# Expert rows of a mixture-of-experts layer: scaled and added in memory into two sums per token, in place of being stored singly and summed afterwards

## The reference, cut to what matters

```
scores = sigmoid(hf @ router_w);  e_idx = top-8 of the masked, biased scores
gate   = scores at e_idx, divided by their sum, * 2.5
yb     = (silu(xb @ w_gate[e]) * (xb @ w_up[e])) @ w_down[e]      # 128-row blocks, one expert each
routed = segment_sum(yb * row_gate, row_tok)                      # 8 rows per token
ffn    = routed + (silu(hf @ sh_gate) * (hf @ sh_up)) @ sh_down
x      = layer_norm(1.189 * x + g2 * ffn) * ln2_g + ln2_b
```

## Time and profile before

| | |
|---|---|
| three timed runs, median (lowest to highest) | 3164.0 us (3163.98 to 3166.07) |
| profiled execution: its own time | 3163.8 us |
| its span, first to last instruction | 3162.2 us |
| mean granted TensorE clock | 0.989 of full speed |
| PE busy; VectorE; ScalarE; GpSimd | 97%; 59%; 18%; 8% |
| DMA traffic | 566.57 MB, mean 179 GB/s |

### The profile page before, as it was taken

The page is one execution under the profiler, slowest core; times in us unless marked ns, Lnnn a source line. Parts: engine busy times, 40 slices in busy tenths (PEclk is TensorE's granted clock), DMA queues, the critical chain, the costliest instruction groups (busy, mean ns, idle before and its releaser), DMA issues. The chain is left out here.

```text
span 3162.2 us, 39915 instructions
## 1 busy us (share of the span) xinstructions
PE 3057.7 (97%) x12530; PEld 1759.4 (56%) x12531; DVE 1856.5 (59%) x3939; ACT 561.5 (18%) x1282; POOL 245.3 (8%) x377
## 2 busy tenths in 40 slices
PE   7999999999999899999998898999999999999998
PEld 4765667644437433333333444478844688588543
DVE  6766676666537644334333567665557755665667
ACT  1002222210002122222221225410000233200000
POOL 1000000011100122222222100000000000000000
PEclk9999999999999999999999999999999999999999
DMA  7673232378762479999997521122254334122342
GB/s 224 198 225 95 66 100 60 107 252 274 242 227 100 149 310 384 378 390 402 370 369 274 214 80 54 41 74 102 85 186 160 100 81 134 54 100 80 135 184 106
DMA packets 270692, 566.57 MB, mean 179 GB/s; under 512 B 27017, under 2 KB 162804, under 8 KB 245994
## 3 DMA queue, kind: packets, MB, share of 16 engines
q1 hardware_dynamic: 213712, 413.72, 36.9%
q0 software_dynamic: 46992, 140.43, 12.7%
q10 hardware_dynamic: 9866, 10.82, 1.0%
HBM read 554.22 MB, written 36.83 MB: 187 GB/s over the span
## 5 line engine op out<-in xcount | busy, mean ns | idle before, releaser
L1522 PE MATMUL ps<-WR,hT 128*64 x832 | 373.7, 603 | 22.8 <-issue 20.7
L1523 PE MATMUL ps<-WR,hT 128*64 128x512 f32 x832 | 373.7, 603 | 0.0
L1967 PE MATMUL ps<-WR 128*128 128x512 f32 x784 | 337.4, 592 | 1.0 <-DVEq L3572 0.7
L1522 PEld LDWEIGHTS ps<-WR,hT 128*64 128x64 f32 x832 | 115.2, 139 | 264.9 <-issue 264.9
L1967 PEld LDWEIGHTS ps<-WR 128*128 128x128 f32 x784 | 148.6, 190 | 188.9 <-issue 186.0
L1161 PE MATMUL ps<-hT,WR 128*128 128x512 f32 x512 | 225.5, 596 | 0.6 <-DVE WR L2813 0.6
L3284 DVE COPY WR<-WR 128x1024 f32 x208 | 131.0, 693 | 160.4 <-SPq L756 110.6
L1926 PE MATMUL ps<-WR 128*128 128x256 f32 x960 | 217.0, 379 | 0.0
L1926 PEld LDWEIGHTS ps<-WR 128*128 128x128 f32 x960 | 182.4, 190 | 24.8
L1543 PE MATMUL ps<-WR 128*64 x416 | 189.5, 598 | 2.7 <-DVEq L3297 1.8
L1544 PE MATMUL ps<-WR 128*64 128x512 f32 x416 | 189.7, 598 | 0.0
(11 more groups left out here) (483 smaller groups left out, 4699.3 us busy)
## 6 DMA issues: line engine op xcount, KB each, us to landing
WR<-in_w_gate SPq DMA_DIRECT2D x64, 1024.0 KB, 8.4
WR<-in_w_up SPq DMA_DIRECT2D x64, 1024.0 KB, 10.8
WR<-in_w_down SPq DMA_DIRECT2D x64, 1024.0 KB, 9.9
WR<-in_mlp_w SPq DMA_DIRECT2D x56, 1024.0 KB, 6.8
WR<-in_mlp_w SPq DMA_DIRECT2D x20, 2048.0 KB, 8.4
xr<-in_ada_w POOLq DMA_DIRECT2D x32, 1024.0 KB, 5.6
WR<-in_w_in SPq DMA_DIRECT2D x56, 512.0 KB, 7.0
xr<-in_w_ada POOLq DMA_DIRECT2D x16, 1024.0 KB, 5.6
```

What stands on the lines that cost most here:

```text
L1522: mm(out[0:HALF], xT[u][:, k, 0:HALF], wa[:, :, k, :], start=(k == 0), stop=(k == KD - 1))
L1523: last = mm(out[HALF:P], xT[u][:, k, HALF:P], wb[:, :, k, :], start=(k == 0), stop=(k == KD - 1))
L1967: return mm(ps[:, bank, :], rows, weights, start=(row == 0), stop=(row == PAST[phase] - 1))
```

## The change

`y_rows` with its 4096 rows goes. In its place is `y_sum`, two rows per token: the first for what rows 0 to 63 of the turns bring, the second for rows 64 to 127 (`half_c` adds the offset). Within one turn each half is one expert's, so no token stands twice in a half. `put` still issues an indirect DMA, now with `compute_op=ALU.add`: it adds each row to the row in memory. The code lets no two additions be under way at once: in `put(1)` GpSimd waits for put(0)'s addition to land, issues its own, and waits for that to land too, before the next pair's gather.

The gate is applied on the way: `put` fetches the 128 gates of its turn with a small indirect DMA from `gate_dram` (a second index column, `pair_c`), and ScalarE's copy out of the accumulator takes them as its `scale`. The table of gates is written to DRAM once ahead of the loop, and 4 MB of zeros are written to `y_sum` while the router runs.

Behind the loop 8 loads of 512 KB replace 32, PE adds both rows of a token through the identity matrix (4 matmuls a tile in place of 8), the shared expert's product of three tiles stands ahead of the wait for the rows, VectorE adds no row at all, and its four token tiles now go one after the other ahead of the four multiplications with the norm's weights.

```diff
-        y_rows = nc.dram_tensor("y_rows", (T * PER_TOKEN, D), F32, kind="Internal").ap()
+        y_sum = nc.dram_tensor("y_sum", (ACC * T, D), F32, kind="Internal").ap()
+        gate_dram = nc.dram_tensor("gate_dram", (T * PER_TOKEN, 1), F32, kind="Internal").ap()
...
+            pool.dma_start(y_sum.rearrange("(r p) d -> p r d", p=P), blank.unsqueeze(1).to_broadcast(
+                [P, ACC * TT, D])).then_inc(sem("y_blank"), 16)
...
-            def put(u, column, n):
+            def put(u, column, n, more=True):
                 ahead(pool, "moe_y_free", n - 1)
                 pool.sem_inc(sem("put_c"), 1)
                 pool.tensor_copy(put_c[u].bitcast(I32), put_i[:, bass.ds(column, 1)].bitcast(I32)).then_inc(
                     sem("put_c"), 1)
-                pool.wait_ge(sem("put_c"), n * 3 + 2)
+                if more:
+                    pool.tensor_copy(pair_c[u].bitcast(I32), pair_i[:, bass.ds(column, 1)].bitcast(I32)).then_inc(
+                        sem("put_c"), 1)
...
+                pool.wait_ge(sem("put_c"), n * 6 + 3)
                 pool.sem_inc(sem("put_c"), 1)
-                pool.indirect_dma_start(y_rows, bass.IndirectOffsetOnAxis(ap=put_c[u].bitcast(I32), axis=0),
-                                        ybuf[u], None, bounds_check=T * PER_TOKEN - 1,
-                                        oob_is_err=False).then_inc(sem(f"y_out{u}"), 16)
+                if more:
+                    pool.indirect_dma_start(gate_c[u], None, gate_dram,
+                                            bass.IndirectOffsetOnAxis(ap=pair_c[u].bitcast(I32), axis=0),
+                                            bounds_check=T * PER_TOKEN - 1, oob_is_err=False).then_inc(
+                                                sem(f"gate_in{u}"), 16)
+                if u == 1:
+                    pool.wait_ge(sem("y_out0"), (n >> 1) * 16 + 16)
+                pool.sem_inc(sem("put_c"), 1)
+                pool.indirect_dma_start(y_sum, bass.IndirectOffsetOnAxis(ap=put_c[u].bitcast(I32), axis=0),
+                                        ybuf[u], None, bounds_check=ACC * T - 1,
+                                        oob_is_err=False, compute_op=ALU.add).then_inc(sem(f"y_out{u}"), 16)
+                if u == 1:
+                    pool.wait_ge(sem("y_out1"), (n >> 1) * 16 + 16)
+                pool.sem_inc(sem("put_c"), 1)
...
             gather(1, idle * 2 + 1, 1)
+            pool.wait_ge(sem("route_v"), ROUTE_V["gates"])
+            pool.dma_start(gate_dram.rearrange("(t p j) o -> p t (j o)", p=P, j=PER_TOKEN), gate8).then_inc(
+                sem("gates_out"), 16)
+            pool.wait_ge(sem("gates_out"), 16)
+            pool.wait_ge(sem("y_blank"), 16)
...
-                pool.dma_start(yg[n % YG], y_of[t, j]).then_inc(sem(f"yg_in{n % YG}"), 16)
-                if n == YG - 1:
+            for t in range(TT):
+                for i in range(ACC):
+                    pool.dma_start(y_in[t][i], y_sum[i * T + t * P:i * T + (t + 1) * P, :]).then_inc(
+                        sem(f"y_in{t}"), 16)
+                if t == 0:
                     pool.dma_start(grow[:, :], row(1)).then_inc(sem("ln_in"), 16)
                     pool.dma_start(lngb[:, 1, :], a["ln2_b"][0].partition_broadcast(P)).then_inc(sem("ln_in"), 16)
...
             def ffn_rows(t):
+                pe.wait_ge(sem(f"y_in{t}"), 16 * ACC)
+                for i in range(ACC):
+                    for n in range(2):
+                        last = mm(ps[:, 2 * t + n, :], ident[:, :], y_in[t][i][:, 512 * n:512 * n + 512],
+                                  start=False, stop=(i == ACC - 1))
                 last.then_inc(sem("ffn_p"), 1)
-                for j in range(PE_ROWS):
...
             def turn_y(u, h):
                 ahead(act, "moe_y", h + 1)
                 act.wait_ge(sem(f"y_out{u}"), (h >> 1) * 16 + 16)
-                A(ybuf[u], ps[:, 5:7, :].rearrange("p b c -> p (b c)"), ACT.Copy).then_inc(sem("moe_y_free"), 1)
+                act.wait_ge(sem(f"gate_in{u}"), (h >> 1) * 16 + 16)
+                A(ybuf[u], ps[:, 5:7, :].rearrange("p b c -> p (b c)"), ACT.Copy, scale=gate_c[u]).then_inc(
+                    sem("moe_y_free"), 1)
...
             def combined(t):
-                dve.wait_ge(sem("ffn_p"), ffn_done(t, PE_ROWS))
-                for j in range(PE_ROWS, PER_TOKEN):
...
+                dve.wait_ge(sem("ffn_p"), t + 1)
+                return ps[:, 2 * t:2 * t + 2, :].rearrange("p b c -> p (b c)")
```

More of the change, by code:

```diff
@@ L131 @@
 ROUTE_P = dict(router_p=1, counts_p=2, ranks_p=3, ends_p=4, first_p=5, tiles_p=6, table_p=7, rows_p=8)
-ROUTE_V = dict(chosen=1, before=2, sums=3, starts=4, ends=5, slots=6, tile_e=7, onehot=8, stack=8 + TT, row_i=9 + TT)
+ROUTE_V = dict(chosen=1, before=2, sums=3, starts=4, ends=5, slots=6, tile_e=7, onehot=8, stack=8 + TT, row_i=9 + TT, gates=10 + TT)
 ADA_SHORT = dict(sum=4 + 1, p=1, free=2, into=(0, 0), bufs=2)
@@ L310, with program @@
 ]
-def program(nc, a, onehot, counting, out):
+def program(nc, a, onehot, counting, blank, out):
     ctx = ExitStack()
@@ L476, in program @@
         fold = view(R, 20588, TURNS)
+        pair_i = view(R, 20460, TURNS)
+        pair_c = [view(R, 20524 + i, 1) for i in range(2)]
+        gate_c = [view(R, 20526 + i, 1) for i in range(2)]
+        half_c = view(R, 20528, 1)
         gate8 = view(R, 18724, TT, PER_TOKEN)
@@ L526, in program @@
         modx = view(R, 19968, 9 * ADA_C)
-        yg = [view(R, D * i, D) for i in range(YG)]
-        gate_diag = view(R, 16384, TT * PE_ROWS, P)
+        y_in = [[view(R, D * (ACC * t + i) if t < TT - 1 else 8192 + D * i, D) for i in range(ACC)] for t in range(TT)]
         ada0 = [view(R, 512 * i, 512) for i in range(4)]
@@ L3061, in residual @@
                     return
-                for t in range(TT + behind):
-                    if t < TT:
+                if branch is not None:
+                    for t in range(TT):
                         branch_in(t)
+                    for t in range(TT):
+                        gained(t)
+                    return
+                for t in range(TT):
+                    branch_in(t)
                     if sums is not None and t == TT - 1:
                         first_sums(sums)
-                    if t >= behind:
-                        gained(t - behind)
+                    gained(t)
             def weight_sums(layer, i):
@@ L3260, in _ @@
             dve.wait_ge(sem("route_p"), ROUTE_P["rows_p"])
+            link.mark(V.memset(half_c[0:HALF, :], 0.5 - PER_TOKEN / 2))
+            link.mark(V.memset(half_c[HALF:P, :], 0.5 - PER_TOKEN / 2 + T * PER_TOKEN))
+            for u in range(2):
+                link.mark(V.memset(gate_c[u], 0.0))
             pair = past_e
@@ L3265, in _ @@
             link.mark(V.tensor_scalar(put_i[:, 0:2].bitcast(I32), pair[:, 0:2], 0.0, float(NO_ROW), ALU.mult, ALU.add))
-            link.mark(V.tensor_copy(put_i[:, 2:2 + TURNS].bitcast(I32), pair))
+            link.mark(V.tensor_scalar(put_i[:, 2:2 + TURNS].bitcast(I32), pair, half_c, 1.0 / PER_TOKEN, ALU.add, ALU.mult))
+            link.mark(V.tensor_copy(pair_i.bitcast(I32), pair))
             link.wait()
@@ L3708 @@
     arrays["counting"] = counting_rows()
+    arrays["blank"] = np.zeros((P, D), np.float32)
     counting = nc.dram_tensor("counting", (P, COUNTS), F32, kind="ExternalInput").ap()
+    blank = nc.dram_tensor("blank", (P, D), F32, kind="ExternalInput").ap()
     out = nc.dram_tensor("out", (1, T, D), F32, kind="ExternalOutput").ap()
[L3711 removed]
+    program(nc, aps, onehot, counting, blank, out)
     r = run_bass_kernel_spmd(nc, [arrays], core_ids=[0])
```

59 lines of the change are left out of this document (15 added, 44 removed).

## The result

The changed kernel takes 3191.4 us (median of 4 runs, 3189.1 to 3202.3) against 3164.0 us before (3160.2 to 3166.1): a ratio of 1.0095 with a 95% interval of [1.0069, 1.0120], so 27.4 us or 0.9% slower. Forecast were 3214 us, slower. The profiled execution took 3189.6 us, its span 3187.9.

The account below looks back on a forecast made before the run. The prediction took the loop to be bound by PE with the weight transfers close behind. From 3163.8 us it subtracted 29.3 saved behind the loop and added 79.2 lost in it: 3213.7, given as 3214, range 3130 to 3335.

Parts of the forecast that it names:

- GpSimd's ring: In the loop: GpSimd's instructions and landings in series for a pair of turns, 5.7 + 2X, 27.7 us; 79 us lost.
- data part: In the loop: a put's landing time beyond an empty put's, 6.7 us of 8.8.
- X: In the loop: time from an addition's issue to its landing, taken as 11.0 us, bounds 8.8 and 15.5.
- PE's stops for weights are inside that, as the weights now arrive ahead: In the loop: PE's waits for weights add nothing beyond the 79 us lost to GpSimd's ring.
- The DMA engines become the bound: Rival, in the loop: second reads fill the engines, 26 us lost against 29 saved, 3161 us; chance 0.13.
- the break-even at X = 9.96: Whole kernel: the X at which loss in the loop equals saving behind it; one microsecond in X is worth 48.
- The additions fit: Rival, in the loop: X stays at a put's 8.8 and the loop keeps its pace, 3134.5 us; chance 0.25.
- the doubled data part: In the loop: the skill's two-reads rule applied to landing makes X 15.5, 266 us lost; full-cost rival's chance 0.17.
- Behind the loop: 23.4 saved, 29.3 forecast: After the loop, up to PE's next projection: fewer loads and sums save 29.3 us, between 24 and 32.
- The last addition is issued where the last put is: At the loop's end: issue at 1705.40 as before, landing 1.5 us later than a put, loads from 1713.0.
- The shared product of three tiles is hidden in PE's wait: Behind the loop: the shared expert's product costs no time, as PE is waiting for rows.
- `grow` ... is late next: Behind the loop: VectorE's multiplication by g2 must wait for `grow`, landing 1722 to 1723, taken as 1723.

Follow-up runs that it names:

- e2: Changed kernel with its additions made plain writes, so a sum holds only its last row; waits and gate fetch stay: 3135.1 us, ratio 0.9916.
- e7: Changed kernel with rows and sums in bfloat16, and the pair's second addition waited for only before the next pair's first addition: 3130.7 us, ratio 0.9900.
- e8: As e7, also without gate fetch and ScalarE's scale, so sums are of unscaled rows: 3129.3 us, ratio 0.9890.
- e10: Kernel before the change with rows in bfloat16, plain puts and 32 loads behind the loop: 3155.6 us, ratio 0.9975.
- e1: Changed kernel with the pair's second addition waited for before the next pair's first addition, no longer before its gather: 3163.7 us, ratio 1.0007.
- e4: Changed kernel with two sums for each buffer, four per token, GpSimd waiting for no landing, 16 tiles added behind the loop: 3183.2 us, ratio 1.0074.
- e5: Changed kernel with e1's moved wait and without gate fetch and scale, so sums are of unscaled rows: 3165.1 us, ratio 1.0008.
- e9: Changed kernel with each gate fetch issued behind its addition, no longer ahead of it: 3169.4 us, ratio 1.0024.
- e3: Changed kernel without the gate fetch, its index copy and ScalarE's scale, so sums are of unscaled rows: 3167.1 us, ratio 1.0013.
- e6: Changed kernel with rows and sums in bfloat16, its waits and gate fetch kept: 3136.9 us, ratio 0.9922.
- the late wait: The edit of e1 to the changed kernel: second addition waited for before the next pair's first addition, not its gather; alone 3163.7 us.

## Why it came out so

The change is slower as forecast, by 27 us and not by 50. The stated range, 3130 to 3335, held times of both signs, so what counts is the mechanism.

**The loop: right mechanism, wrong size, and a second bound beside the first.** Three limits show in the runs.

- PE with the weights close behind: 24.1 to 24.4 us (before, e2, e7, e8, e10).
- The DMA engines with the additions' second read in float32: 25.6 (e1, e4, e5), whatever gates there are. GpSimd waits for PE here and hardly for a landing.
- GpSimd's ring: 26.97 in the changed kernel.

The ring's parts, means of the 23 pairs that the pace is taken from. They add up to the pace because they cut it without a gap; what matters is which of them change.

| run | own part: copy to buffer 0's addition, us | to buffer 1's addition | to the next pair's copy | pace |
|---|---|---|---|---|
| changed | 5.12 | 11.28 | 10.58 | 26.97 |
| e9 gate behind | 3.72 | 11.20 | 10.75 | 25.67 |
| e3 no gate fetch | 3.60 | 11.49 | 10.80 | 25.89 |
| e6 half bytes | 5.18 | 9.74 | 9.55 | 24.47 |
| e2 plain write | 5.02 | 9.96 | 9.31 | 24.29 |

The pair shown above, with 5.55, has one of the longest own parts, and the one ahead of it (28.3 us) is no exception: 8 of the 23 take 28 us or more, three take less than 24.1. Buffer 1's additions land after 9.7 us in the mean, and GpSimd's next copy starts 0.85 us behind the landing.

Do the bounds combine as a maximum? Not exactly. In e9 the own part is 1.4 us shorter and the pace 1.30, nearly one for one, so the ring still sets many pairs; e1, which has no ring, is only 0.06 faster. The two waits in the table of runs tell the same: PE's for gathers goes from 40.6 to 21.7 in e9 and to nothing in e1, while VectorE's for weights goes from 120.4 to 136.2 and 163.6. As the first bound goes, the second takes its place; in e9 both hold some pairs. That the second exists is shown by e1, e4 and e5, and that it is the bytes by e7.

PE's clock is a smaller matter. Between 1150 and 1650 a matmul is busy for 204.6 ns in the mean before (484.94 us for 2370), 206.6 in e1 and 211.6 in the changed kernel (460.44 us for 2176). That is some 0.2 us a pair in e1 of the 1.2 lost, and some 0.8 in the changed kernel, where GpSimd's waits are for landings all the same.

The step that was mis-sized is "a third of the data part on top, **X = 11.0**, is what I take". X measured 10.2, a fifth of the data part (1.4 of 6.7). By the forecast's own formula that gives 5.7 + 20.4 = 26.1 and 24 x 1.7 = 41 us, against 79 forecast and 49 measured. The constant was too small at the same time: 5.7 forecast, 5.12 + 2 x 0.85 = 6.8 measured, as the reaction to a landing takes 0.85 us and not 0.6, and the own part is 5.12 where 2.07 + 2.4 stood. The two errors work against each other, so that the forecast ring of 27.7 comes so near to 26.97 is partly luck.

The loss isn't 24 times the ring's surplus either. The 49.0 are 1.1 at the start, 23 x 2.57 = 59.3 in between, and 11.3 given back after the 25th addition (39.9 us to the last copy, 51.2 before). The rows show what that is: the additions fall behind ScalarE's copies and catch up. The second addition of buffer 0 is issued 4.4 us behind the copy that it carries (ended at 1088.23), the 25th 14.6 us behind (1698.43); before, both puts stood 1.5 behind. After the 25th no gather of a next pair stands in the ring, its own part is down to 2.5 us (1731.54 to 1734.07), and the last two pairs are done in 21.1 and 16.2 us. Counted at the copies, from the first to the 26th of buffer 0, the pace is 26.35 us against 24.32: 25 x 2.03 = 50.8, less the 1.8 us by which the first copy ends earlier. (52 gathers and 26 copies of each buffer stand in both traces, so 52 turns carry rows, where 54 stand ahead of the prediction.)

**"PE's stops for weights are inside that, as the weights now arrive ahead": wrong.** VectorE's wait for them did not shrink (120.4 us for 110.6), and without the ring it grew to 163.6 (e1). The rival *The DMA engines become the bound* had the arithmetic that e1 confirmed: 44 us of engine time, 18 in the gaps, 26 lost, 3161 us; e1, e4 and e5 lost 24.4 to 26.5, e1 took 3163.7. It was written as an alternative, but it is a floor under the forecast: at 25.6 us a pair even a landing of 8.8 us would have left the loop 24 us longer, so the break-even at X = 9.96 gives no gain with float32 rows. (A slip in the same list: at X = 13.5 the formula gives 3334, not 3329.) e2 shows the rival *The additions fit* (3134.5 forecast, 3135.1 measured), but only with the reads taken away.

**The engines' time, from rows.** In e8 GpSimd's queue took 14.7% of 500 us for 41 turns, 1.79 us a turn; in e10, with plain puts, 10.6% or 1.29. The kernel before had 13.8%, 1.68 a turn, gather and put of equal bytes, so I estimate 0.84 for each. Then a put in bfloat16 is 0.45 and an addition 0.95, 2.1 times as much. In float32, e5 has 20.5% for 39 turns, 2.63 a turn: an addition is 1.79, again 2.1 times a put's 0.84. That is 1.9 us more a pair. The engines' share was 0.97 between 1150 and 1650, so their slack (0.03 of 24.4 us) takes 0.7; 1.2 remain, and 1.2 were measured. The match is closer than the estimate deserves, since the share in e1 is 0.98 and not 1.00. In bfloat16 the surplus is 1.0 a pair: with e10's share of 0.95 it fits in the slack, and e8's pace is e10's within 0.06.

The Trainium skill, Collectives: The Full Stack, section "The bandwidth ceiling: the fold count and why AG ≠ RS ≠ AR", says of a collective's reduce step that its add emits two source reads and halves the rate. By engine time these runs agree, with 2.1 times by the estimate above; by time to landing they don't: 10.2 us where the doubled data part would give 15.5. The prediction applied the rule to the landing; its place was the engines' share.

**Behind the loop: 23.4 saved, 29.3 forecast.** "The last addition is issued where the last put is" failed, and is 2.6 us of the 5.9: it waits 4.24 us for the one in front of it, which is the same wait that the loop's ring is made of. Loads begin 11.8 us behind the loop's end and not 9.2, VectorE's first product (1775.51) 22.7 and not 19.2, the tiles take 6.5 us each where 6.37 stood. PE's projection follows VectorE's last root step (1801.26 + 0.16) by 12.6 us instead of 10.5; its first 8 sums took 5.63 us, not 3.6, behind 6.30 us of idling, with a granted clock of 0.66 between 1769 and 1776. "The shared product of three tiles is hidden in PE's wait" held. "`grow` ... is late next" did not: it landed 6.6 us behind its issue, at 1772.5, and VectorE's first product followed PE's sums, which ended at 1775.47:

```profile
1775.51 1.23 DVE L3045 TENSOR_TENSOR WR<-ps,grow 128x1024 f32<-128x1024 f32 x1 [28.11 <-PE ps L1603]
```

**Ahead of the loop: nothing, as forecast.** The second addition of buffer 0 stands 1.07 us later than the put did, and the first copy of that buffer ends 1.8 us earlier.

## What to carry to other kernels

When a change puts waits in series and adds traffic, work out each resource's time for one turn of the loop and take the longest as the least that it can take; where two lie close, both hold some turns (e9). Relief of one shows only down to the next, and a rival with a lower cost may be a floor under the forecast instead of an alternative to it. In a ring of landings, look at what an engine issues between a landing and the next start: moving one small fetch out of there was worth some 20 us. Mean parts over many turns, and not one turn's rows, say how long the ring is. Where adding in memory saves work later, halve its bytes or make room on the DMA engines first: with bfloat16 rows and the late wait it made this kernel 1.0% faster, in float32 it just broke even (e1, e5).

## What was not expected of the hardware

- An addition in memory lands only 1.4 us later than a write of the same rows (10.2 against 8.8 in the middle of the loop), but takes 2.1 times the DMA engines' time, by the estimate above. GpSimd's issue takes 1.6 us instead of 1.0.
- A fetch of 128 values of four bytes lands in 5.6 us in the loop (median, e1), two thirds of a 0.33 MB gather's 9.0 there, and costs nothing in the pace when nobody's ring holds it (e5 against e1).
- From the landing of an addition that GpSimd waits for to the start of its next instruction pass 0.85 us in the mean (changed kernel, 23 pairs).
- Halving the bytes of an addition shortened its landing by only 1.1 us (10.2 to 9.1).
- Halving the bytes of the loads behind the loop (e10) shortened that part by 0.3 us of 84.5.
